# Activations beside their remainders for products of 512 columns, and expert slots picked head by head, in a two-block decoder kernel

## The reference

```python
# first_block, per layer l (modulated by c): attention, then
h = rms_norm(x, norm_ffn[l]) * (1 + sc_f) + sh_f
x = x + g_f * ((silu(h @ w_gate[l]) * (h @ w_up[l])) @ w_down[l])     # D_FF = 2816
# second_block, per layer l: head_group_mixer, memory_cross_attn, then peer_ffn:
q = (h @ w_pq).reshape(B, S, 8, 2, 128)                               # 8 heads, two halves
scores = einsum('bshpd,hpkd->bshpk', q, sub_keys)                     # 128 keys in each half
top_s, top_i = top_k(scores, 16)
cand_s = (top_s[..., 0, :, None] + top_s[..., 1, None, :]).reshape(B, S, 8, 256)
cand_i = (top_i[..., 0, :, None] * 128 + top_i[..., 1, None, :]).reshape(B, S, 8, 256)
best_s, best_pos = top_k(cand_s, 16)
expert_idx = take_along_axis(cand_i, best_pos, axis=-1)
gate = softmax(best_s, axis=-1)
a = einsum('cd,chkd->chk', hc, expert_u[expert_idx])                  # 16384 experts
out = einsum('chk,chkd->cd', gate * gelu(a), expert_v[expert_idx])
```

## Time and profile before

| what | value |
|---|---|
| median of 3 runs | 2908.13 us (2906.12 to 2909.43) |
| profiled execution | 2918.25 us, its span 2916.5 us |
| PE busy | 2818.6 us (97%) |
| DVE busy | 1971.7 us (68%) |
| ACT busy | 1336.6 us (46%) |
| read from HBM | 527 MB, 183 GB/s over the span |

### The profile page before, as it was taken

The page is one execution under the profiler, slowest core; times in us unless marked ns, Lnnn a source line. Parts: engine busy times, 40 slices in busy tenths (PEclk is TensorE's granted clock), DMA queues, the critical chain, the costliest instruction groups (busy, mean ns, idle before and its releaser), DMA issues.

```text
span 2916.5 us, 45834 instructions
## 1 busy us (share of the span) xinstructions
PE 2818.6 (97%) x19604; PEld 2547.9 (87%) x19604; DVE 1971.7 (68%) x2790; ACT 1336.6 (46%) x1454; POOL 194.7 (7%) x168
## 2 busy tenths in 40 slices
PE   7889999999999899999999999998999999999998
PEld 6768998789988789999988888897899999988887
DVE  6767766664443558877769965535589777699755
ACT  3454435554457444443434444484444534344443
POOL 0200002010003000220000000030000500000000
PEclk9989999999999999999999999999999999999999
DMA  7848864645543345554445555533455544455554
GB/s 294 292 147 303 306 214 148 213 173 188 185 182 130 130 157 176 174 188 160 173 154 193 174 188 193 217 130 118 156 174 177 185 163 170 160 188 174 188 191 148
DMA packets 75658, 537.78 MB, mean 184 GB/s; under 512 B 8512, under 2 KB 8896, under 8 KB 12096
## 3 DMA queue, kind: packets, MB, share of 16 engines
q1 hardware_dynamic: 75456, 534.86, 52.0%
HBM read 527.48 MB, written 7.34 MB: 183 GB/s over the span
## 4 chain that ended last, share of the span: by engine, by line
PE 63%; issue 22%; DVE 6%; POOL 3%; ACT 3%; DMA 2%; SPq 0%; DVEq 0%; POOLq 0%; ACTq 0%
PE bank L401 10%; PE bank L411 10%; PE bank L403 10%; PE bank L453 7%; PE bank L455 6%; PE bank L463 6%; POOL big L2165 2%; PE bank L427 2%; PE bank L429 2%; PE bank L438 2%; DVE wlo L1329 2%; PE bank L491 2%; DMA raw<-in_wkv 1%; PE bank L838 1%; ACT whi L891 1%
## 5 line engine op out<-in xcount | busy, mean ns | idle before, releaser
L891 ACT ACTIVATE whi<-raw 128x2048 fp32r<-128x2048 f32 x438 | 839.3, 1917 | 1073.2 <-PE bank L403 544.8
L1329 DVE TENSOR_TENSOR wlo<-raw,whi 128x2048 fp32r<-128x2048 f32 x438 | 1007.8, 2301 | 424.4 <-ACT whi L891 424.0
L401 PE MATMUL bank<-hth,whi 128*128 128x256 f32 x3392 | 835.1, 286 | 3.4 <-DVE htl L1399 1.9
L403 PE MATMUL bank<-htl,whi 128*128 128x256 f32 x3392 | 824.7, 283 | 0.0
L401 PEld LDWEIGHTS bank<-hth,whi 128*128 128x128 f32 x3392 | 649.4, 191 | 8.7 <-DVE htl L1394 3.3
L403 PEld LDWEIGHTS bank<-htl,whi 128*128 128x128 f32 x3392 | 650.0, 192 | 1.2 <-issue 0.5
L453 PE MATMUL bank<-whi,hth 128*128 128x512 f32 x1152 | 459.1, 399 | 14.4 <-DVE htl L1394 10.0
L455 PE MATMUL bank<-whi,htl 128*128 128x512 f32 x1152 | 451.9, 392 | 0.0
L411 PE MATMUL bank<-hth,wlo 128*128 128x256 f32 x3392 | 441.9, 283 | 1.0 <-DVE wlo L1329 1.0
L411 PEld LDWEIGHTS bank<-hth,wlo 128*128 128x128 f32 x3392 | 422.2, 192 | 1.4 <-DVE wlo L1329 1.4
L463 PE MATMUL bank<-wlo,hth 128*128 128x512 f32 x1152 | 287.4, 389 | 0.0
(11 more groups left out here) (255 smaller groups left out, 2978.8 us busy)
## 6 DMA issues: line engine op xcount, KB each, us to landing
raw<-in_pu SPq DMA_DIRECT2D x128, 1024.0 KB, 4.8
raw<-in_pv SPq DMA_DIRECT2D x128, 1024.0 KB, 4.8
raw<-in_win SPq DMA_DIRECT2D x52, 1024.0 KB, 4.8
big<-in_wmod SPq DMA_DIRECT2D x24, 1024.0 KB, 7.2
raw<-in_wmod SPq DMA_DIRECT2D x24, 1024.0 KB, 5.2
raw<-in_wgate SPq DMA_DIRECT2D x22, 1024.0 KB, 4.9
raw<-in_wup SPq DMA_DIRECT2D x22, 1024.0 KB, 5.0
raw<-in_wdown SPq DMA_DIRECT2D x22, 1024.0 KB, 4.9
```

The source lines that it names most:

```text
L401: e.matmul(o[n], h[:, q, c[n]], H[:, q * 256:(q + 1) * 256], start=n == 0 and q == 0, stop=False, skip_group_check=True)
L403: m = e.matmul(o[n], h[:, q, c[n]], L[:, q * 256:(q + 1) * 256], start=False, stop=False, skip_group_check=True)
L891: e.activation(whi(j), slot[u][0], ACT.Copy).then_inc(*hi.mark(j))
L1329: e.tensor_tensor(wlo(j), slot[u][0], whi(j).bitcast(F32), ALU.subtract).then_inc(*lo.mark(j))
```

## The change

**Tiles.** `HTH` and `HTL` become one tile `HT` in which 256 columns of high activations are followed by the 256 columns of their remainders (`Halves`: `.both`, `.hi`, `.lo`); the same for `HID` and `MT`. The eight PSUM banks become one tensor.

**`wide_unit`.** It replaces `a_unit` for the gate and up units, the cross queries, pq and pu: 44 + 8 + 16 + 128 = 196 units in all (the memory keys and the second mixer's column units stay `a_unit`). The high weights are multiplied by high and low activations in one matmul of 512 columns, 16 of them, one bank for each group of 128 output columns; the 16 matmuls with the low weights stay at 256 columns. A unit now takes a pair of banks (4 and 5, or 6 and 7; `Banks.pair`), so two units can be in flight. The product is then the sum of the two halves of a bank: ACT copies the first halves (`apart`), DVE adds the second halves (`joined`), and only then come Silu or Gelu, in place in SBUF, and for the feed-forward the product of gate and up, in SBUF too.

**Selection.** `select_slots` and the new `slots_summed` do the comparison, the POOL multiplication and the sums head by head, for both halves of the tokens, in tiles of 128x512, and the sums of a head come one head later. The softmax of the gates is one Exp in place of two, `exponents` at unit 30 and `shares` at unit 31. The budgets of `some` become 3.0 in a pq step after the first two and 2.4 in the pu units 0 to 29. The transposes move from unit 29 to unit 32 (`GATES`), the one-hot groups start at 32, and every fourth unit has two groups in place of every eighth.

```diff
+class Halves:
+    def __init__(self, x):
+        v = x.rearrange("p (c h n) -> p c h n", h=2, n=256)
+        self.both, self.hi, self.lo = x, v[:, :, 0], v[:, :, 1]
...
+    def pair(self, key):
+        self.turn += self.turn % 2
+        b = 4 + self.turn % 4
+        self.turn += 2
+        before = [self.held.get(b), self.held.get(b + 1)]
...
     def pace(u):
-        return 2 if u % 8 == 2 else 1
+        return 2 if u % 4 == 0 else 1
...
+        def wide_unit(key, M, ready, between=None):
+            k = take()
+            b, held = banks.pair(key)
...
+            for n in range(2):
+                evicted(held[n])
+                for q in range(8):
+                    if n == 0 and q % 2 == 0:
+                        ready(q // 2)
+                    m = e.matmul(bank[b + n], h[:, q, c[n]], M.both[:, q * 512:(q + 1) * 512], start=q == 0, stop=False,
+                                 skip_group_check=True)
+                if n == 0 and between is not None:
+                    between()
+            m.then_inc(*hi_read.mark(k))
+            on.wait_ge(*lo.at(k))
+            for n in range(2):
+                for q in range(8):
+                    m = e.matmul(bank[b + n][:, 0:256], w[:, q, c[n]], M.hi[:, q], start=False, stop=q == 7,
+                                 skip_group_check=True)
...
-                a_unit(("a", l, u), HTH, HTL, ready, between)
+                wide_unit(("a", l, u), HT, ready, between)
...
+        def apart(dst, key, k):
+            on.wait_ge(*unit.at(k))
+            e.copy(pair(dst), parts(key)[0]).then_inc(*took_a.mark(key))
...
+            def gelu(u):
+                x = ag(u * 512, 512)
+                on.wait_ge(*took_v.at(("a", l, u)))
+                e.activation(x, x, ACT.Gelu).then_inc(*a_soft.mark(("gelu", l, u)))
             for u in range(64):
-                if u in (21, 25):
-                    exponent(u // 25)
+                if u == GATES - 1:
+                    exponent()
                 k = take()
                 upto(k + 2)
-                on.wait_ge(*unit.at(k))
+                if u:
+                    gelu(u - 1)
                 region(on, l, u)
-                key = ("a", l, u)
-                e.activation(ag(u * 512, 512), psum(key)[:, :], ACT.Gelu).then_inc(*took_a.mark(key))
+                apart(ag(u * 512, 512), ("a", l, u), k)
+            gelu(63)
...
+        def joined(dst, key):
+            on.wait_ge(*took_a.at(key))
+            e.tensor_tensor(pair(dst), parts(key)[1], pair(dst), ALU.add).then_inc(*took_v.mark(key))
...
         def selection(l):
             for h in range(8):
                 yield from select_head(l, h)
-            for t in range(2):
-                yield from select_slots(l, t)
+                if h:
+                    yield from slots_summed(l, h - 1)
+                yield from select_slots(l, h)
...
                 if i:
-                    some(2.2)
+                    joined(ag(QT + (i - 1) * 512, 512), ("pq", l, i - 1))
+                    some(3.0 if i > 1 else 0.0)
...
                 take()
+                if u:
+                    activated(u - 1)
+                if u == GATES - 2:
+                    some(1e9)
+                    exponents(l)
+                if u == GATES - 1:
+                    shares(l)
+                if u == GATES:
+                    slots_turned(l, 0)
+                    slots_turned(l, 1)
...
-                if u < 29:
-                    some(2.7)
+                if u < GATES - 2:
+                    some(2.4)
```

More of the change, by code:

```diff
@@ L25 @@
 NRAW = 3
+GATES = 32
 NSP = 2
@@ L91, in take @@
         self.held[b] = key
+        self.where[key] = b
+        return b, before
+    def pair(self, key):
[3 more added lines that the diff above has]
+        before = [self.held.get(b), self.held.get(b + 1)]
+        self.held[b] = self.held[b + 1] = key
         self.where[key] = b
@@ L188, in program @@
     IOTAH = at("iotah", 204800 + 4 * 1888, 128, F16)
-    bank = [ctx.enter_context(nc.psum_tensor(f"bank{i}", [P, 512], F32)) for i in range(8)]
+    PS = ctx.enter_context(nc.psum_tensor("banks", [P, 4096], F32))
+    bank = [PS[:, i * 512:(i + 1) * 512] for i in range(8)]
     banks = Banks()
@@ L194, in psum, with parts, pair @@
         return bank[banks.where.get(key, 0)]
+    def parts(key):
+        b = banks.where.get(key, 0)
+        v = PS[:, b * 512:(b + 2) * 512].rearrange("p (n h c) -> p n h c", n=2, h=2)
+        return v[:, :, 0], v[:, :, 1]
+    def pair(x):
+        return x.rearrange("p (c n) -> p c n", n=256)
     def ag(o, n):
@@ L353, in tensor, with evicted @@
         used = [0]
-        def clear(key, b=None):
-            b, held = banks.take(key, b)
+        def evicted(held):
             if took_a.has(held):
@@ L360, in clear @@
                 on.wait_ge(*took_v.at(held))
+        def clear(key, b=None):
+            b, held = banks.take(key, b)
+            evicted(held)
             return b
@@ L389, in take, with a_unit @@
             return k
-        def a_unit(key, H, L, ready, between=None, b=None):
+        def wide_unit(key, M, ready, between=None):
+            k = take()
+            b, held = banks.pair(key)
+            h, w = whi(k).rearrange("p (k n) -> p k n", k=8), wlo(k).rearrange("p (k n) -> p k n", k=8)
+            c = [slice(n * 128, (n + 1) * 128) for n in range(2)]
+            for n in range(2):
[13 more added lines that the diff above has]
+                                 skip_group_check=True)
+            m.then_inc(*unit.mark(k))
+            return k
+        def a_unit(key, M, ready, between=None, b=None):
             k = take()
@@ L414, in a_unit, with b_unit @@
             return k
-        def b_unit(keys, H, L, half, ready, b=(None, None), between=None):
+        def b_unit(keys, M, half, ready, b=(None, None), between=None):
             k = take()
@@ L816, in peer @@
                 if i < 8:
-                    a_unit(("pq", l, i), HTH, HTL, ready)
+                    wide_unit(("pq", l, i), HT, ready)
                 if i:
@@ L1094, in feed_forward @@
             for i in range(11):
+                gate, hd = (ag(PR + 1024 * x + (i % 2) * 512, 512) for x in range(2))
                 k = take()
                 upto(k + 2)
-                on.wait_ge(*unit.at(k))
                 if i >= 2:
@@ L1198, in query @@
                 key = ("xq", l, h)
[L1199 removed]
                 since()
[L1201 removed]
+                apart(ag(QTX + h * 512, 512), key, k)
                 last_h[0] = k
@@ L1865, in selection, with slots_summed @@
+        def slots_summed(l, h):
+            for w in range(2):
+                on.wait_ge(*p_mul.at((l, "pick", h, w)))
+                dst = ag(II, 768).rearrange("p (t w k) -> p t w k", t=2, w=3)[:, :, w, h * 16:(h + 1) * 16]
+                e.tensor_reduce(dst, picked(h, w), X, ALU.add).then_inc(*top.mark((l, "red", h, w)))
+                yield 0.65
         def selection(l):
```

306 lines of the change are left out of this document (149 added, 157 removed).

## The result

| | span of the profiled execution | timed, median | runs |
|---|---|---|---|
| before | 2916.5 us | 2918.73 us (2906.12 to 2926.42) | 20 |
| changed | 2905.3 us | 2905.76 us (2898.33 to 2910.44) | 20 |

The changed kernel takes 0.9963 of the time before, with a 95% interval of 0.9953 to 0.9974: 11 us faster where 31 were forecast. The time lies above the range of 2867 to 2897. The forecast in absolute time started from the three timed runs of before that were known then, median 2908.13 us; over twenty runs the median is 2918.73, so 10.6 us of the distance to the forecast of 2877 are in the starting value. From 2908.1 the measured ratio gives 2897.4, just past the end of the range; the missing gain is the same from either start.

A forecast was written before the change was run, and what follows sets the result against it. PE was taken to bound the kernel, with DVE close behind in the selection. 42.1 + 1.0 - 2.0 - 5.2 - 2.6 - 1.4 - 0.7 = 31.2 us saved gave 2877 us timed, range 2867 to 2897.

The forecast's parts named there:

- wide matmuls, 196 units: On PE, 512 columns save a matmul's fixed 0.0134 us once: 0.215 us a unit, 42.1 us saved.
- pq to pu: At the stage end, pu's start waits for DVE's addition: 0.7 us a layer, 1.4 us lost.
- one-hot groups: In the one-hot stage DVE's extra addition is covered: 5.66 us a unit against about 6.1 on PE; no cost.
- slot turn: At the slot transposes, unit 32 needs unit 31's pair of banks: PE waits 2.6 us a layer, 5.2 us lost.
- pu to pv: At the stage end, copy and addition come ahead of Gelu: 1.3 us a layer (1.1 to 1.5), 2.6 us lost.
- selection on DVE: In pu during the selection, dear steps make PE wait: 1.0 us a layer (0 to 2.7), 2.0 us lost.
- waits of units 26 to 29: In the selection, unit 26's 0.49 us wait for a late split goes away in both layers: 1.0 us back.
- cross attention: The last addition stands ahead of the third head's maxima: at most 0.69 us a layer, half taken, 0.7 us lost.
- The rival on the width: On PE, a wide matmul takes 0.2394 us and saves nothing: 2919 us, slower; chance 0.04.
- The other two rivals, on DVE in the selection: DVE becomes the bound through POOL's bursts, 2894 us, chance 0.14; or the selection overruns far, 2924 us, chance 0.05.
- the prediction's own signs of being wrong: Wide matmuls over 0.23 us apart; PE often waiting for `joined`; splits of 2.8 us; other stage-end waits over 1 us each.
- they will wait for the addition, 0.7 a layer: From pq to pu, PE's last score products and pu wait for DVE's addition: 1.4 us lost in all.

The follow-up runs named there:

- the run of the hand-over from pq to pu: Changed kernel with no selection steps between the additions of the seventh and eighth pq, 6.0 us of them after the eighth; 0.9928 of before.
- three waits mended: Changed kernel with slot transposes in separate banks, no selection steps between the last two pq additions, first pv weights split before Gelu 62; 0.9865 of before, 2880.9 us.

## Why the prediction was wrong

By its own terms, in us over both layers. Lengths of units are distances between first matmuls of neighbouring units in the two profiled executions.

| term | forecast | found | difference in gain |
|---|---|---|---|
| wide matmuls, 196 units | 42.1 | 0.19 a unit: 37.2 | -4.9 |
| pq to pu | 1.4 | 10.73 for 7.59 us, with the width 3.3 a layer: 6.6 | **-5.2** |
| score products behind each pq | 0 | a unit with its scores 0.07 shorter, not 0.19: 1.7 | -1.7 |
| one-hot groups | 0 | the 32 groups lengthen their units by 18.2 a layer (one 0.59, two 1.06), before by 17.2 (0.55, 1.01): 2.0 | -2.0 |
| slot turn | 5.2 | 3.53 behind unit 31, less 0.58 for transposes that were there: 5.9 | -0.7 |
| pu to pv | 2.6 | 9.58 for 7.90, with the width 1.87 a layer: 3.7 | -1.1 |
| selection on DVE | 2.0 | 0 | +2.0 |
| waits of units 26 to 29 | 1.0 back | 0.86 a layer: 1.7 back | +0.7 |
| cross attention | 0.7 | 0.5 | +0.2 |
| sum of the terms | 31.2 | 18.5 | -12.7 |
| half clock behind the waits | not in the sum | 7.7 | **-7.7** |

18.5 stands against 18.9 in the traces; the 0.4 us left are within what two executions of one kernel differ by (1.6).

- **What was right.** The mechanism and its place: PE the bound, the fixed part of a matmul saved once. The rival on the width is refuted: doubling the columns costs 0.107 us, so 13 ns are fixed. The Trainium skill's rule that I set against it (page "TensorE: Matmul & The Clock Gate", section "Back-to-back issue gap") would have given, as an estimate, 8 us; the 34 to 37 measured speak for the trace. I had also read the page too broadly: it gives this rule for a single matmul by itself, and for a stream with weight loads it names 131 ns at 512 columns, which the 227 ns here do not bear out either. The other two rivals, on DVE in the selection, did not come either: 30 units stand at 5.57 us without a wait, though DVE is busy for 97% of that stretch. The slot turn was priced nearly right (2.95 us a layer for 2.6). Of the prediction's own signs of being wrong one came: a wait of over 1 us at another stage end.
- **The step that failed most in the sum** is "they will wait for the addition, 0.7 a layer". It priced the hand-over at 0.7 us a layer where it took 3.3. The 0.7 is the time of the addition and not the time at which DVE gets to it. Before, the last copy of pq was ACT's, and ACT was free. Now DVE must add, and DVE's program has a piece of the selection, 3.0 us planned, ahead of it. The chain in layer 0: ACT's copy is done at 1103.14, the addition begins at 1105.79, PE goes on at 1106.52.

```profile
1102.56 0.58 ACT L971 COPY big<-banks 128x512 f32<-128x512 f32 x1 [3.17 <-PE banks L436]
...
1105.79 0.67 DVE L1462 TENSOR_TENSOR big<-banks,big 128x512 f32<-128x512 f32 x1
...
1106.52 1.16 PE L875 MATMUL banks<-big 128*128 128x128 f32 x8 [2.99 <-DVE big L1462]
```

- **From pu to pv** a step was left out of the chain: 1.3 us a layer were forecast (1.1 to 1.5), 1.87 were found. The Gelu of unit 62 stands on ACT ahead of the copy of unit 63, 0.52 us from start to start. PE's last pu matmul ends at 1487.31 in layer 0; then:

```profile
1487.31 0.61 ACT L1325 ACTIVATE big<-big 128x512 f32<-128x512 f32 x1
1487.83 0.56 ACT L971 COPY big<-banks 128x512 f32<-128x512 f32 x1
1488.43 0.69 DVE L1462 TENSOR_TENSOR big<-banks,big 128x512 f32<-128x512 f32 x1 [3.67 <-ACT big L971]
1489.15 0.63 ACT L1325 ACTIVATE big<-big 128x512 f32<-128x512 f32 x1 [0.76 <-DVE big L1462]
...
1491.17 0.76 PE L503 MATMUL banks<-whi,ht 128*128 128x512 f32 x1 [3.85 <-DVE ht L1457]
```

- **The width** was mis-sized by 0.025 us a unit. Count over time in a stretch gave 0.2260 for 512 columns; between two starts it is 0.227 inside a unit, and the first matmul of each half takes a little more, so a unit is 5.57 and not 5.53. 196 times a fortieth is 5 us.
- **The step that was missing**, and the largest single item, is the price of standing still: a term that the prediction put at nothing without a reason. Each wait was counted with its own length alone. Behind a wait of 2.7 to 3.9 us the clock fell at five of the six places of the changed kernel, in both of its profiles, and each fall costs 1.5 to 1.7 us more. The trace of before had it: behind the wait of the earlier trace rows in layer 0 the first unit of pv took 8.07 us, in layer 1, behind the same wait, 6.51. I had read the granted clock only in stretches where PE was full, and there it is 1.00. One of the microseconds of that first unit, in layer 0 before the change, has 0.50:

```profile
1502.00:1503.00 1.00, 1.00 (x3) 0.81 (x4) 1.00 (x4) 0.00 (x0) 0.00 (x0) 0.50 0.00 0
```

The Trainium skill states it on the page "TensorE: Matmul & The Clock Gate", in the section "Part 1: The HAM clock gate": PE's clock goes to half when PE has been idle, and where the change comes varies, since the chip's monitor does not run in step with the kernel. The traces agree: 0.50 and 1.00 are the levels, and a wait of the same length is followed by a fall at one place and not at another (the 3.0 us from pq to pu in the changed kernel: layer 1 and not layer 0; the slot turn: both layers of the changed kernel, neither in the run of the hand-over from pq to pu). But it is not free chance from one execution to the next either: in both executions of the changed kernel it was the same five places of six.

## What to carry to other kernels

When an engine's work moves to another engine, price the hand-over by what stands ahead of it in the new engine's program and not by the operation's own length. Read every wait of PE with the granted clock of the microseconds behind it: here a wait of 2.7 us cost 4.3. Where a wait can't be mended, idle matmuls into a free bank kept the clock at each of the twelve places where that was tried, and the waits did not grow, since they ended before the waits did.

## What the runs showed of the hardware

- With transposes of a 128x128 identity in 32 bits, 0.113 us apart, at the start of a wait of 2.7 to 4.3 us, the granted clock stayed at 1.00 at twelve places of twelve, with 1.3 to 1.7 us of stillness left at the end of eleven of them and 2.6 at one (second mixer of layer 0). Without them the clock fell at five of the first six places (changed kernel, both executions) and at four of the other six (three waits mended, one execution).
- Waits shorter than these can be followed by a fall too: 1.98 us in layer 0 of the kernel before. Behind the waits of 1.5 us that were left from pu to pv there was none (two kernels, two layers), nor behind those of 2.5 and 2.6 us there and before unit 2 of pu in the two runs that had them.
- The loss at half clock differs between profiled executions by up to 9 us at places whose code is the same (second mixer: 3.4 us in each layer in one execution, none in another). Not every fall costs 1.5 to 1.7 us: at the start of the second peer layer it was 3.1 in the profile with the three waits mended. The clock is also most of the spread of the timed runs: over the 38 runs of before (2909 to 2930 us) the time rises by 2.4 us with each 0.001 of granted clock that is missing; all runs under 2913 us have 0.985 to 0.987, all over 2923.5 us 0.979 to 0.982.
